# Second layer's mixture of three attention groups: another order of its weights, one product on GpSimd, another queue for the key roots

## What is computed

```python
for g, (window, dilation) in enumerate(DSA_PATTERNS):        # ((128, 1), (512, 4), (2048, 16))
    o, lse = _dilated_window_attention(q[:, :, g], k[:, :, g], v[:, :, g], window, dilation)
    outs.append(o); lses.append(lse)
wts = jax.nn.softmax(jnp.stack(lses), axis=0)
o = jnp.einsum('gbsh,gbshd->bshd', wts, jnp.stack(outs))     # the mixture
...
y_a = (o_a * jax.nn.silu(dsa_z)) @ w_up_a[layer]             # the mixture, gated
gk = _l2norm(gk.reshape(b, s, GDN_HEADS, GDN_KEY_DIM))       # keys over their roots
beta = jax.nn.sigmoid(gdn_b.astype(f32))
o_b = _gated_delta_rule(gq, gk, gv, g, beta)                 # uses k * beta, exp of summed log decays
```

## Time and profile before

| | |
|---|---|
| Runs | 2786.97, 2789.36, 2793.34 us |
| The profiled execution's own time | 2792.05 us |
| Its span in the trace | 2790.3 us |
| Busy: TensorE, VectorE, ScalarE, GpSimd | 96%, 53%, 35%, 7% of the span |
| The stretch that the change touches | about 2425 to 2485 us of the span |

### The profile page before, as it was taken

The page is one execution under the profiler, slowest core; times in us unless marked ns, Lnnn a source line. Parts: engine busy times, 40 slices in busy tenths (PEclk is TensorE's granted clock), DMA queues, the critical chain, the costliest instruction groups (busy, mean ns, idle before and its releaser), DMA issues.

```text
span 2790.3 us, 42160 instructions
## 1 busy us (share of the span) xinstructions
PE 2690.6 (96%) x17668; PEld 2212.2 (79%) x17668; DVE 1489.0 (53%) x1850; ACT 965.1 (35%) x1472; POOL 206.2 (7%) x284
## 2 busy tenths in 40 slices
PE   6999999999999999999999999999999999978998
PEld 5888878787888887888877787888878777768787
DVE  6555575765565434333356754333355565775644
ACT  3222233623222233222335433222233544533332
POOL 3000000220000000000000410000000000043000
PEclk9999999999999999999999999999999999988999
DMA  7566552102556322233222102232233331240222
GB/s 296 188 215 218 172 187 91 65 3 98 211 192 223 126 95 89 86 103 105 83 91 79 33 32 83 89 107 90 91 101 127 104 106 68 87 116 4 69 94 76
DMA packets 53370, 313.41 MB, mean 112 GB/s; under 512 B 7617, under 2 KB 7745, under 8 KB 24929
## 3 DMA queue, kind: packets, MB, share of 16 engines
q1 hardware_dynamic: 41760, 236.65, 24.9%
q0 software_dynamic: 11456, 74.55, 7.9%
HBM read 302.69 MB, written 2.20 MB: 109 GB/s over the span
## 4 chain that ended last, share of the span: by engine, by line
PE 91%; DVE 5%; DMA 2%; ACT 1%; issue 1%; POOL 0%; SPq 0%; DVEq 0%; ACTq 0%
PE ps L971 18%; PE ps L972 18%; PE ps L973 18%; PE ps L1259 6%; PE ps L1260 6%; PE ps L1261 6%; PE ps L2130 1%; PE ps L2114 1%; PE ps L2127 1%; PE ps L1526 1%; PE ps L1528 1%; PE ps L1527 1%; DMA ada_first<-in_ada 1%; DVE w_lo L947 1%; PE ps L1341 1%; PE ps L1996 1%
## 5 line engine op out<-in xcount | busy, mean ns | idle before, releaser
L971 PE MATMUL ps<-hn_hi,w_hi 128*128 128x512 f32 x1440 | 564.9, 392 | 16.6 <-DVE hn_lo L920 16.6
L972 PE MATMUL ps<-hn_lo,w_hi 128*128 128x512 f32 x1440 | 563.9, 392 | 0.0
L973 PE MATMUL ps<-hn_hi,w_lo 128*128 128x512 f32 x1440 | 563.8, 392 | 0.0
L947 DVE TENSOR_TENSOR w_lo<-w_raw,w_hi 128x2048 fp32r<-128x2048 f32 (+2 forms) x227 | 467.9, 2061 | 163.0 <-ACT w_hi L940 162.9
L940 ACT ACTIVATE w_hi<-w_raw 128x2048 fp32r<-128x2048 f32 (+2 forms) x227 | 390.7, 1721 | 94.0 <-PE ps L1261 90.6
L971 PEld LDWEIGHTS ps<-hn_hi,w_hi 128*128 128x128 f32 x1440 | 272.8, 189 | 75.5 <-issue 18.4
L1259 PE MATMUL ps<-hn_hi,w_hi 128*128 128x512 f32 x776 | 316.3, 408 | 15.6 <-DVE spare L1454 7.0
L972 PEld LDWEIGHTS ps<-hn_lo,w_hi 128*128 128x128 f32 x1440 | 272.8, 189 | 56.8
L973 PEld LDWEIGHTS ps<-hn_hi,w_lo 128*128 128x128 f32 x1440 | 272.5, 189 | 56.9
L1260 PE MATMUL ps<-hn_lo,w_hi 128*128 128x512 f32 x776 | 307.8, 397 | 0.0
L1261 PE MATMUL ps<-hn_hi,w_lo 128*128 128x512 f32 x776 | 307.3, 396 | 0.0
(11 more groups left out here) (461 smaller groups left out, 3518.3 us busy)
## 6 DMA issues: line engine op xcount, KB each, us to landing
w_raw<-in_up SPq DMA_DIRECT2D x88, 1024.0 KB, 4.8
ada_w<-in_ada POOLq DMA_DIRECT2D x64, 1024.0 KB, 5.1
w_raw<-in_down SPq DMA_DIRECT2D x64, 704.0 KB, 4.1
w_raw<-in_mix_in SPq DMA_DIRECT2D x20, 1024.0 KB, 4.8
w_raw<-in_dsa_in SPq DMA_DIRECT2D x18, 1024.0 KB, 5.2
w_raw<-in_merge SPq DMA_DIRECT2D x16, 768.0 KB, 4.2
ada_first<-in_ada SPq DMA_DIRECT2D x8, 1024.0 KB, 12.3
w_raw<-in_mix_out SPq DMA_DIRECT2D x8, 1024.0 KB, 4.9
```

The source lines that it names most:

```text
L947: dve.tensor_tensor(w_lo[:, slot, 0:size], w_raw[:, slot, 0:size], w_hi[:, slot, 0:size].bitcast(F32), ALU.subtract).then_inc(w_lo_ready, 1)
L971: pe.matmul(bank, wh, x_hi[:, k], start=(k == 0), stop=False)
L972: pe.matmul(bank, wh, x_lo[:, k], start=False, stop=False)
L973: return pe.matmul(bank, wl, x_hi[:, k], start=False, stop=(k == K - 1))
```

## The change

The order of the three groups, the engines and the queues change, and with them the tiles that hold the spread rows:

- Group 2's weights are spread first and group 1's second; group 0's come third, once the other two products have been added.
- GpSimd multiplies group 1 (`mix_product`), four instructions of 128x512, once that group's weights have landed. VectorE multiplies group 2, adds the two products in `row_spread[1]`, and multiplies and adds group 0 at the end. Count 4 of `dsa_mixed` now means a finished mixture, and the gate on GpSimd waits for it.
- All three small writes of head rows stand behind the second spread. The roots are then spread by ScalarE's queue into tiles of their own (`root_spread`), in front of the silu of `dsa_z`. The betas are spread into `gd_qd`, ahead of group 0's weights, and `gd_qd` takes the read decays only after `gd_normed`.
- VectorE takes the first half of `ds_z` out of PSUM before the reciprocal of the sums instead of behind the weights.
- Two waits change their form without moving an instruction: `dsa_sine` becomes the engine's own counter, and `gd_decayed` is counted together with `gd_read_ready`.

```diff
+        root_spread = tiles("root_spread", 40, 4)
...
+        def mix_product(eng, group, j):
+
+            d = DILATION[group]
+            w = row_spread[group % 2][:, j].rearrange("p (i r) -> p i r", r=d)
+            return eng.tensor_tensor(w, ds_q[group][:, j].rearrange("p (r i) -> p i r", r=d), w, ALU.mult)
...
         def spread_rows_pool(pool):
 
             pool.wait_ge(dsa_weights, 1)
             pool.dma_start(mix_rows[:], ds_max[0:8]).then_inc(rows_out, 16)
             pool.wait_ge(rows_out, 16)
-            mix_spread_pool(pool, 0, 0)
+            mix_spread_pool(pool, 0, 2)
             pool.wait_ge(gd_sums, 4)
             mix_spread_pool(pool, 1, 1)
-            pool.wait_ge(gd_roots, 1)
+            pool.wait_ge(gd_k_rooted, 1)
+            pool.dma_start(gd_head_rows[0], gd_rows[32:40, 1]).then_inc(rows_out, 16)
             pool.dma_start(gd_head_rows[1], gd_rows[0:8, 0]).then_inc(rows_out, 16)
             pool.dma_start(gd_head_rows[2], restart[32:40]).then_inc(rows_out, 16)
+            pool.wait_ge(row_spread_in[1], 64)
+            for j in range(PAIRS):
+                mix_product(pool, 1, j).then_inc(dsa_weighted, 1)
+            gd_e_pool(pool, 0)
+            pool.wait_ge(rows_out, 64)
             pool.wait_ge(dsa_mixed, 1)
-            mix_spread_pool(pool, 0, 2)
-            pool.wait_ge(gd_k_rooted, 1)
-            pool.dma_start(gd_head_rows[0], gd_rows[32:40, 1]).then_inc(rows_out, 16)
-            pool.wait_ge(rows_out, 64)
+            head_spread(pool, gd_qd, 1, gd_betas_in)
             pool.wait_ge(dsa_mixed, 2)
-            head_spread_pool(pool, row_spread[1], 0, row_spread_in[1])
-            head_spread_pool(pool, gd_kbg, 2, gd_decays_in[1])
-            gd_e_pool(pool, 0)
-            pool.wait_ge(dsa_mixed, 3)
-            head_spread_pool(pool, row_spread[0], 1, row_spread_in[0])
-            head_spread_pool(pool, gd_qd, 2, gd_decays_in[0])
+            mix_spread_pool(pool, 0, 0)
+            pool.wait_ge(dsa_weighted, PAIRS)
+            head_spread(pool, gd_kbg, 2, gd_decays_in[1])
+            pool.wait_ge(gd_normed, 2)
+            head_spread(pool, gd_qd, 2, gd_decays_in[0])
 
         def gated_pool(pool):
 
+            pool.wait_ge(dsa_mixed, 4)
             pool.wait_ge(dsa_z_ready, 1)
             pool.tensor_tensor(ds_q[0][:], ds_q[0][:], ds_z[:], ALU.mult).then_inc(ya_f_ready, 1)
...
             act.activation(gd_q[:], gd_v[:], ACT.Silu).then_inc(act_own, 1)
+            act.wait_ge(rows_out, 64)
+            act.wait_ge(act_own, 3)
+            head_spread(act, root_spread, 0, gd_roots_in)
             act.wait_ge(dve_evac, pz + 2)
...
+            second_evac_dve(dve, pz, ds_z[:, 1:2])
             own(dve.reciprocal(r[:, 3], r[:, 3]))
             dve.tensor_tensor(mx, mx, r[:, 3:4].broadcast_to([8, 3, T]), ALU.mult).then_inc(dsa_weights, 1)
-            second_evac_dve(dve, pz, ds_z[:, 1:2])
             split_dve(dve, *whole(pg))
             dve.wait_ge(gd_roots, 1)
             dve.reciprocal(g_rows[:, 1], g_rows[:, 1]).then_inc(gd_k_rooted, 1)
-            mix_group_dve(dve, own, 0)
             second_evac_dve(dve, pz + 1, ds_z[:, 3:4])
             split_dve(dve, *whole(pg + 1))
-            mix_group_dve(dve, own, 1)
-            mix_group_dve(dve, own, 2)
+            dve.wait_ge(row_spread_in[0], 64)
+            for j in range(PAIRS):
+                last = mix_product(dve, 2, j)
+            last.then_inc(dsa_mixed, 1)
+            dve.wait_ge(dsa_mixed, 1)
+            dve.wait_ge(dsa_weighted, PAIRS)
+            dve.tensor_tensor(row_spread[1][:], row_spread[1][:], row_spread[0][:], ALU.add).then_inc(dsa_mixed, 1)
             second_evac_dve(dve, pg, gz(1).rearrange("p (a t) -> p a t", a=1))
-            dve.wait_ge(row_spread_in[1], 96)
-            dve.tensor_tensor(gd_k[:], gd_k[:], row_spread[1][:], ALU.mult).then_inc(gd_k_normed, 1)
-            dve.wait_ge(row_spread_in[0], 160)
+            dve.wait_ge(gd_roots_in, 32)
+            dve.tensor_tensor(gd_k[:], gd_k[:], root_spread[:], ALU.mult).then_inc(gd_k_normed, 1)
+            dve.wait_ge(row_spread_in[0], 128)
+            dve.tensor_tensor(ds_q[0][:], ds_q[0][:], row_spread[0][:], ALU.mult).then_inc(dsa_mixed, 1)
+            dve.wait_ge(dsa_mixed, 3)
+            dve.tensor_tensor(ds_q[0][:], ds_q[0][:], row_spread[1][:], ALU.add).then_inc(dsa_mixed, 1)
+            dve.wait_ge(gd_betas_in, 32)
             dve.wait_ge(gd_k_normed, 1)
+            dve.wait_ge(dsa_mixed, 4)
             for b in range(2):
                 pair = slice(2 * b, 2 * b + 2)
-                dve.tensor_tensor(gd_kq[:, 0, pair], gd_k[:, pair], row_spread[0][:, pair], ALU.mult).then_inc(gd_normed, 1)
+                dve.tensor_tensor(gd_kq[:, 0, pair], gd_k[:, pair], gd_qd[:, pair], ALU.mult).then_inc(gd_normed, 1)
             split_dve(dve, *whole(pm))
```

31 lines of the change are left out of this document (8 added, 23 removed).

## The result

| | before | changed |
|---|---|---|
| Median of the runs | 2791.93 us (8 runs, 2786.97 to 2793.42) | 2799.26 us (8 runs, 2798.31 to 2800.63) |
| Ratio | | 1.0028, 95% interval 1.0019 to 1.0038 |
| The profiled execution: own time, span | 2792.05, 2790.3 us | 2798.39, 2796.3 us |

The change makes the kernel 0.28% slower by the ratio, 7.3 us (0.26%) by the medians, where 8.0 us were forecast. The forecast time, 2797.4 us, had the shorter series before, with its median of 2789.36, as its base.

What follows compares the result with a forecast made beforehand. The prediction took the chain of weight spreads, mixture and `gd_kq` ahead of the delta rule's first mask as the bound. Keys 4.9 us late plus 3.1 us of uncovered gate gave 2789.4 + 8.0 = 2797.4 us, range 2791 to 2802.5.

Steps and rivals of the forecast that it cites:

- GpSimd's product: Group 1's four strided products on GpSimd: 1.91 us each, 7.7 us together, bounds 5.1 to 10.2.
- When group 1 lands: Landing of group 1's weights spread: 2451.3 instead of 2449.65, from 0.6 us for a copy and 1.0 for a load.
- the 1.0 for the load: A 768 KB weight load now beside group 1's spread delays its landing by 1.0 us, bounds 0 and 1.9.
- The masks: The decays' masks on GpSimd, 2.5 us, now between its product and the betas' spread, ending at 2461.6.
- this stall costs nothing: VectorE's sum of groups 1 and 2, even if held by GpSimd, is ready by about 2464, while betas still move.
- Betas and group 0 in a row: Two 1 MB spreads, one behind the other on GpSimd's queue, take 11.9 us; group 0 lands at 2473.5.
- rival 2: Spreads of betas and group 0 move at 414 GB/s instead of 217; 3.4 us late, 2792.8 us; chance 0.08.
- The gate: On GpSimd behind a spread waiting for `gd_normed`, the gate loses its cover and delays the first mask by 3.1 us.
- What was costed at nothing: Waits and transfers off the path, among them roots on ScalarE's queue and piece pg+1 on TensorE: 0 us.
- Rival 1: GpSimd does not mind the stride: its product takes 5.1 us, first mask 5.4 us late, 2794.8 us; chance 0.17.
- rival 3: Cheap stride, fast spreads and full TensorE clock at the delta rule's first step, 1.9 us back; 2788.3 us; chance 0.07.
- Rival 4: GpSimd and VectorE collide in product or gate, and the load costs 1.9 us: up to 13 us late, 2802.4; chance 0.18.

Runs made afterwards that it cites:

- e8: The kernel before with one edit: the read decays' spread waits for `gd_normed`, so the gate starts after the keys; 2792.02 us, ratio 1.0006 to before.
- e9: The changed kernel with the split of piece pg+1 moved back behind group 2's product, so the next load of weights starts later; 2798.32 us, one run.
- e5: The changed kernel with group 1's product on GpSimd reading its outputs contiguously, leaving out the reordering of tokens; 2798.25 us, one run.
- e1: The changed kernel with the read decays spread by ScalarE's queue, so GpSimd's gate stands directly behind the mixture; 2798.03 us, ratio 1.0026 to before.
- either order alone: The changed kernel with either group 0's weights ahead of the betas (2794.70 us) or the decays' masks ahead of GpSimd's product (2795.44 us).
- both together: The changed kernel with group 0's weights ahead of the betas and the decays' masks ahead of GpSimd's product; 2791.82 us, ratio 1.0003 to before.

## Why the prediction was right, step by step

The sign, the place and the size held: the first mask was forecast at 2486.4 and came at 2486.26, shifted. But this agreement of 0.1 us is luck: errors of -1.5 and -1.6 us were made good by one of +2.1 and three small ones. Of the signs that I had named, group 0 near 2473 and the gate behind `gd_kq` with the mask waiting for it came true; GpSimd's products near 1.9 us (1.53) and their start from 2450 on (2449.92) did not. The steps, each against its shifted time:

| step | forecast | measured | the step's own error |
|---|---|---|---|
| GpSimd's product starts | 2451.4 | 2449.92 | -1.5 |
| it ends | 2459.1 | 2456.03 | -1.6 (6.1 for 7.7 us) |
| the decays' masks end | 2461.6 | 2460.59 | +2.1 (4.6 for 2.5 us) |
| group 0's product starts | 2473.5 | 2472.99 | +0.5 (12.4 for 11.9 us) |
| `gd_kq` ends | 2480.5 | 2480.10 | +0.1 |
| first mask | 2486.4 | 2486.26 | +0.3 (6.2 for 5.9 us) |

- **When group 1 lands: too late by 1.5 us against this execution.** The same landing came 0.4 to 0.9 us later in six other profiles with this queue, and moved by at least 1.6 us in e8 with no cause in its diff. The 0.6 us of the copy came as forecast (the weight rows are written out 1.94 us ahead of the stage's start instead of 2.54); the 1.0 for the load has e9 for it, and not more than that.
- **GpSimd's product: mis-sized.** The step that failed is "on GpSimd this gives 1.91 us each": 1.53 was measured, 1.25 without the stride (e5). The factor of a stride on VectorE did not carry over to GpSimd. The bounds, 5.1 to 10.2, held it.
- **The masks: the step that was wrong in kind.** I wrote that VectorE's sum may be held while GpSimd works and that this stall costs nothing. It does cost VectorE nothing. But this collision held both engines, and GpSimd stands on the path: L620 took 3.33 us, and the betas' issue came 2.1 us later. I read rows 4 and 5 as VectorE being held by GpSimd, because L609 and L610 kept their 1.28 and 1.26 us there.
- **Betas and group 0 in a row: right.** 11.9 us from the last four transfers of before, 12.4 measured, and 225 GB/s with full DMA engines: rival 2, faster spreads, fell with that.
- **The gate: right.** 3.1 us without its cover were forecast, 3.35 measured in e8, in the kernel before with this one edit. That "the gate starts right behind `gd_kq`" is bad for it was right, that it could be hidden there (my theory of e1) was not.
- **What was costed at nothing**: the roots by ScalarE's queue were issued at 2449.24 and caused no wait, and piece pg+1 was done in time; TensorE then waited 12.83 us for the keys.
- **The rivals.** Rival 1 did not hold as stated, 6.11 us against its limit of 5.3, though the stride costs a fifth and not a half; rival 3 fell with the clock at 0.50 and 4.54 us. Rival 4, the collision, was there, at another place than I had looked for it, and with 2.1 of its 5.0 us; e1 shows one at its full price.

Of the 7.83 us in the stage, e8 accounts for 3.35 (the gate). The keys' part, 2480.10 - 2475.6 = 4.5 us, has no single owner: either order alone takes back 4.5 to 5.0, both together 6.0, since what is left is then another wait.
